# Attention with probabilities and values as half precision pairs, and the second half's keys copied in two parts in the third turn

## The chip, the cores and the metric

The kernel runs on one core of a Trainium2 chip. The metric is the time of one execution on the device, in microseconds; the times given are medians of several runs. The engines are named as in the profile: PE (TensorE, the matmuls), PEld (its weight loads, which overlap PE), DVE (VectorE), ACT (ScalarE), POOL (GpSimd) and SP (SyncE, whose queue issues most DMAs).

## What is computed

Two layers of an encoder for 256 prompt tokens and 64 sample tokens (T = 320 together). Each layer has a projection, latent attention with 8 heads, an mLSTM branch, a gated MLP branch, their gated sum, and a mixture of 16 experts. The change touches the attention alone:

```python
def _attend_block(qn, qr, qpos, kn, kr, v, kpos):
    s = jnp.einsum('bqhd,bkhd->bhqk', qn, kn) + jnp.einsum('bqhd,bkd->bhqk', qr, kr)
    s = s.astype(jnp.float32) * ATTN_SCALE
    allowed = (kpos // CHUNK)[None, :] <= (qpos // CHUNK)[:, None]
    s = jnp.where(allowed[None, None], s, -jnp.inf)
    p = jax.nn.softmax(s, axis=-1)
    return jnp.einsum('bhqk,bkhd->bqhd', p.astype(v.dtype), v)
...
    for l in range(DEPTH):
        z = x @ w_in[l] + b_in[l]
        cq, ckv, kr, mq, mk, mv, mi, mf, mo, gu, gv, gt = _split(z)
        q = (_rmsnorm(cq, q_norm_g[l]) @ w_uq[l]).reshape(B, T, MLA_HEADS, NOPE_DIM + ROPE_DIM)
...
        kv = (ckv_all @ w_ukv[l]).reshape(B, past + T, MLA_HEADS, NOPE_DIM + V_DIM)
        a_out = _mla_attention(qn, qr, positions, kv[..., :NOPE_DIM], kr_all, kv[..., NOPE_DIM:], kpos)
...
        merged = jax.nn.sigmoid(gt[..., :D_MODEL]) * (a_out @ w_branch[l, 0])
...
        x = _layernorm(DN_ALPHA * x + merged @ w_out[l], ln1_g[l], ln1_b[l])
        moe_out = _moe(x, router_w, router_b, moe_w_gate[l], moe_w_up[l], moe_w_down[l],
                       shared_w_gate[l], shared_w_up[l], shared_w_down[l])
        x = _layernorm(DN_ALPHA * x + moe_out, ln2_g[l], ln2_b[l])
```

The 256 prompt tokens see only prompt tokens up to their own chunk of 64; the 64 sample tokens see 256 cached tokens and themselves.

## The kernel before

The engines have hand-written programs, joined by semaphores (`Signal`: a semaphore and its count per layer). Activations lie transposed, 128 features on the partitions and the 320 tokens in the free dimension.

**Weights** come as blocks of 128 x 1024 f32, 358 in all, over SP's queue into eight buffers `w32`. ACT writes the upper half of a block's bits as f16 into `whi` (`hi_at`, L555), DVE the rest into `wlo` (`lo_at`, L1074); each has four slots. A matmul of full precision is then three f16 matmuls: hi x hi, hi x lo, lo x hi (`group`, L1777). PE starts a block when DVE's count of low halves reaches it (`ready`), ACT may refill a slot when PE's count `blk_done` has passed it, and SP reloads a `w32` buffer when DVE has read it.

**The attention stage** of a layer has 16 such blocks, A0 to A0 + 15. Blocks 0 and 1 hold the query and key/value projections of heads 0 to 3 ("half 0"), 4 and 5 those of heads 4 to 7 ("half 1"), the other twelve are merge gates, independent of the attention: `gate(a)` is 24 matmuls of 320 columns, and serves as work for PE between the steps of attention. Their results take turns in banks 0 to 3 of the PSUM ("items"); `item_freed` says which copy out of a bank must be done before PE may write it again.

**The loop** has 12 turns, u = 0 to 11. u // 6 is the half, and three turns deal with two heads: u % 3 = 0 and 1 are one head's 256 prompt tokens each, u % 3 = 2 is the 64 sample tokens of both heads (the "short" turn). A unit goes through these steps, each on another engine, with units u, u - 1 and u - 2 under way at once:

- `scores(u)` on PE (L2034, L2041), f32, into bank 4 or 5;
- row maxima on DVE (L1465 to L1470) into `sm`, signal `s_max`;
- `exps(u)` on ACT (L796 to L801): exponentials into `prob`, f32, two buffers, and their sums; signal `p_exp`;
- reciprocal and normalisation on DVE (L1473 to L1481), signal `p_norm`;
- `transposes(u)` on PE (L2051): three f32 transposes into bank 6, signal `t_ps`;
- `probs_out(u)` on ACT (L809 to L814): bank 6 into `prob_t` (in `ysq`), f32, signal `t_sb`;
- `values(u)` on PE (L2068 to L2076), f32, weights `v_kv` (64 wide, one head), into bank 7, signal `o_ps`. After three units `out_hi` (ACT) and `out_lo` (DVE) copy bank 7 into the f16 pair `br_hi`, `br_lo`.

In a turn PE runs scores(u), transposes(u - 1), values(u - 2), and then a block of filler work: `queries(1)` in turn 1, `keys(1)` in turn 2, `vals(1)` in turn 3, a gate block in all others. The copies of these results out of PSUM are `q_out`, `k_out` (four parts of two copies) on ACT, `rotate`, `rotated` and `v_out` on DVE. After the loop come gate(14), transposes(11), values(10), gate(15), values(11), and the branches' output projections, which use bank 0 to 3 in the same way.

## Time and profile before

| | us |
|---|---|
| runs | 1021.13, 1021.45, 1022.71 (median 1021.45) |
| the profiled execution | 1021.76 |
| its span, first to last instruction | 1019.9 |
| PE busy | 979.0 (96%) |
| DVE busy | 806.5 (79%) |
| ACT busy | 655.3 (64%) |
| mean granted PE clock | 0.993 of full speed |

A matmul's record is longer than the time it costs: a matmul of 320 columns has a record of 300 ns, and the next one starts 136 ns later. Costs on PE are therefore read from start to start, or from the chain of work that ended last, where a piece lasts until the next begins. The same holds on a small scale on ACT and DVE, where the next instruction begins some 0.1 us before the record of the last one ends.

### The profile page before, as it was taken

The numbers are of one execution on the slowest core, as the hardware profiler recorded it, in microseconds if no ns is written. First come the engines' busy times: TensorE is split into PE (matmuls) and PEld (weight loads), VectorE is DVE, ScalarE is ACT, GpSimd is POOL, SyncE is SP. The second block draws the span as 40 slices with busy tenths as digits, with TensorE's granted clock in tenths as the row PEclk, the third lists the DMA queues.
The fourth block names the chain that finished last, engine by engine and source line by source line (L and its number), as shares of the span: only waits on it lengthen the run. The fifth ranks groups of instructions, "written<-read, shape, count | busy, mean of one in ns | idle before, by whom it ended". The sixth has DMA issues, their size and how long they took to land.

```text
span 1019.9 us, 24037 instructions
## 1 busy us (share of the span) xinstructions
PE 979.0 (96%) x9862; PEld 757.6 (74%) x9862; DVE 806.5 (79%) x1436; ACT 655.3 (64%) x1057; POOL 0.7 (0%) x10
## 2 busy tenths in 40 slices
PE   8999999999999999999999999999999989999995
PEld 6877777777776799976568777777777768998653
DVE  4796767654689899998888876676448899999986
ACT  5675454754355799876776645556543659987864
POOL 0000000000000000000000000000000000000000
PEclk9999999999999999999999999999999999999998
DMA  9845454423465199998836534442334435999961
GB/s 352 301 170 166 148 151 121 131 83 110 145 222 166 54 322 368 360 361 317 288 125 210 181 124 141 151 146 85 104 124 148 144 102 167 359 364 365 375 233 55
DMA packets 59652, 205.02 MB, mean 201 GB/s; under 512 B 7216, under 2 KB 10348, under 8 KB 59020
## 3 DMA queue, kind: packets, MB, share of 16 engines
q1 hardware_dynamic: 55980, 195.95, 55.8%
q10 hardware_dynamic: 3552, 7.42, 2.1%
q8 instruction: 82, 1.34, 0.5%
q14 instruction: 38, 0.31, 0.1%
HBM read 198.76 MB, written 3.40 MB: 198 GB/s over the span
## 4 chain that ended last, share of the span: by engine, by line
PE 64%; DVE 21%; DVEq 5%; ACT 4%; issue 3%; DMA 1%; SPq 1%; ACTq 0%
PE bank L1777 37%; DVE wlo L1074 12%; PE bank L1801 4%; DVEq L1700 4%; PE bank L2313 3%; ACT whi L555 2%; PE bank L2145 2%; PE bank L1806 1%; PE bank L2000 1%; DMA w<-in_w 1%; DVE mo L1702 1%; PE bank L2034 1%; PE bank L2076 1%; DVE xT L1087 1%; PE bank L2329 1%
## 5 line engine op out<-in xcount | busy, mean ns | idle before, releaser
L1074 DVE SCALAR_TENSOR_TENSOR wlo<-w,whi 128x1024 f16<-128x1024 f32 x358 | 428.9, 1220 | 69.4 <-ACT whi L555 67.9
L555 ACT ACTIVATE whi<-w 128x1024 f16<-128x1024 f32 x358 | 368.8, 1048 | 81.6 <-PE bank L1777 48.1
L1777 PE MATMUL bank<-xhi,whi 128*128 128x320 f16 x688 | 206.2, 300 | 0.7 <-DVE wlo L1074 0.6
L1777 PE MATMUL bank<-xhi,wlo 128*128 128x320 f16 x688 | 205.7, 299 | 0.0
L1777 PE MATMUL bank<-xlo,whi 128*128 128x320 f16 x688 | 205.7, 299 | 0.0
L1777 PE MATMUL bank<-arena_b,whi 128*128 128x112 f16 x2048 | 161.7, 213 | 7.7 <-DVE wlo L1074 6.7
L1777 PEld LDWEIGHTS bank<-arena_b,whi 128*128 128x128 f16 x2048 | 149.5, 98 | 12.8 <-issue 8.6
L1777 PE MATMUL bank<-arena_b,wlo 128*128 128x112 f16 x1024 | 157.3, 213 | 0.0
L1777 PEld LDWEIGHTS bank<-arena_b,wlo 128*128 128x128 f16 x1024 | 100.1, 98 | 0.0
L1777 PEld LDWEIGHTS bank<-xhi,whi 128*128 128x128 f16 x688 | 67.2, 98 | 30.8 <-issue 2.8
L1777 PEld LDWEIGHTS bank<-xhi,wlo 128*128 128x128 f16 x688 | 67.3, 98 | 26.1
L1777 PEld LDWEIGHTS bank<-xlo,whi 128*128 128x128 f16 x688 | 67.4, 98 | 25.6 <-issue 1.4
L1777 PE MATMUL bank<-br_hi,whi 128*128 128x320 f16 x192 | 57.4, 299 | 0.0
L1777 PE MATMUL bank<-br_lo,whi 128*128 128x320 f16 x192 | 57.4, 299 | 0.0
L1777 PE MATMUL bank<-br_hi,wlo 128*128 128x320 f16 x192 | 57.4, 299 | 0.0
L2313 PE MATMUL bank<-whi,arena_a 128*112 128x512 f16 x128 | 48.8, 381 | 1.8 <-DVE wlo L1074 1.8
L2313 PE MATMUL bank<-wlo,arena_a 128*112 128x512 f16 x128 | 48.5, 379 | 0.0
L2313 PE MATMUL bank<-whi,arena_b 128*112 128x512 f16 x128 | 48.5, 379 | 0.0
L1801 PE MATMUL bank<-whi,xhi 128*128 128x128 f16 x256 | 44.9, 222 | 2.6 <-ACT x_tail L628 2.6
L703 ACT ACTIVATE arena_a<-bank,par_h 128x320 f32<-128x320 f32 x24 | 12.6, 526 | 53.8 <-PE bank L1777 53.8
L1801 PE MATMUL bank<-whi,xlo 128*128 128x128 f16 x256 | 45.0, 222 | 0.0
L1801 PE MATMUL bank<-wlo,xhi 128*128 128x128 f16 x256 | 44.9, 222 | 0.0
(378 smaller groups left out, 1747.4 us busy)
## 6 DMA issues: line engine op xcount, KB each, us to landing
w<-in_w SPq DMA_DIRECT2D x358, 512.0 KB, 4.9
arena_b<-head_rows ACTq DMA_DIRECT2D x2, 1920.0 KB, 7.3
xT<-in_x SPq DMA_DIRECT2D x2, 640.0 KB, 5.5
out_y<-xT SPq DMA_DIRECT2D x4, 320.0 KB
rows<-in_rows ACTq DMA_DIRECT2D x1, 1024.0 KB, 10.5
rows<-in_rows SPq DMA_DIRECT2D x1, 1024.0 KB, 5.9
out_ckv<-arena_a SPq DMA_DIRECT2D x2, 320.0 KB
acc<-kr SPq DMA_DIRECT2D x2, 288.0 KB
```

The lines of the kernel that those rows point to most:

```text
L555: A(whi[:, n % SLOTS, :], w32[:, n % RAW, :], ACT.Copy, scale=WS).then_inc(hi_done.sem, 1)
L703: A(dst, bank[(M0 + step) % 4][:, 0:T], func, scale=scale, bias=par_t[:, bass.ds(col, 1)]).then_inc(z_ev.sem, 1)
L1074: V.scalar_tensor_tensor(wlo[:, n % SLOTS, :], w32[:, n % RAW, :], WS, whi[:, n % SLOTS, :], ALU.mult, ALU.subtract).then_inc(lo_done.sem, 1)
L1087: V.scalar_tensor_tensor(xT[:, c * T:(c + 1) * T], acc[:, c * T:(c + 1) * T], par_g[:, gain + c:gain + c + 1], ln_r[:, :], ALU.mult, ALU.m ...
L1700: dve.drain()
L1702: V.tensor_tensor(two(h2[:, 0:W2]), two(h1[:, 0:W2]), bank[4 + 2 * e2][:, 0:CAP].unsqueeze(1).broadcast_to([P, 2, CAP]), ALU.mult).then_in ...
L1777: ins = M(out, w[:, s, sub * P:(sub + 1) * P], rhs(part, k), start=(n == 0), stop=(n == 3 * len(subs) - 1))
L1801: M(bank[b][0:m, i * P:(i + 1) * P], x[:, k, t0:t0 + m], w[:, s, k * P:(k + 1) * P], start=(j == 0), stop=(j == 3 * KD - 1))
L1806: ins = M(bank[b][:, 2 * P:3 * P], x_tail[:, k, :], w[:, s, k * P:(k + 1) * P], start=(k == 0 and w is whi), stop=(k == KD - 1 and w is wlo))
L2000: a = M(b[0:m, (i % 2) * 2 * P:(i % 2 + 1) * 2 * P], x[:, k, i * P:i * P + m], w[:, s1, (4 + 2 * k) * P:(6 + 2 * k) * P], start=(j == 0), ...
L2145: a = M(out_bank(c)[:, 0:T], w[:, slot(l, O0 + c), k * P:(k + 1) * P], m[:, k, :], start=(k == 0 and w is whi and m is mhi), stop=(k == KD ...
L2313: a = M(b[0:CAP, :], h_[:, bass.ds(g * (8 * CAP) + ((2 * q + kt) * CAP + H0), CAP)], w[:, slot(l, n), kt * 512:(kt + 1) * 512], start=(q = ...
```

## The change

Probabilities and values become pairs of f16 numbers, as the weights and activations already are.

- `v_kv` becomes `v_hl`: `v_out` is parted into `v_out_hi` on ACT and `v_out_lo` on DVE. `prob` has one buffer; the normalised probabilities are written as `prob_h` (hi by `probs_hi` on ACT, lo by `probs_lo` on DVE, scaled by 4096), `prob_t` as hi by `columns_hi` on ACT and lo by `columns_lo` on DVE. The normalising passes on DVE go; one on the two reciprocals comes.
- `exps(u)` now also waits for `probs_lo(u - 1)`, which frees `prob`; `transposes(u)` waits for `probs_lo(u)`, `values(u)` for `columns_lo(u)`.
- A transpose is two f16 matmuls against the identity that add up in PSUM, values three f16 matmuls where one f32 was (`weigh`).
- On PE the filler block stands ahead of values(u - 2), and these ahead of transposes(u - 1). On ACT and DVE the copy of a transposed unit moves from the next turn to the start of the one after.
- The copies of half 1 move: `q_out(1)` from turn 2 to the end of turn 1, `k_out(1)` from turn 3 to turn 2 in two parts around exps(2), `rotate(1)` from turn 2 to turn 1, `rotated(1)` ahead of the reciprocal of turn 2. `v_out(1)` stays in turn 4.

```diff
+PS = 4096.0
...
-        v_kv = arena_b[:, 8 * T:16 * T].rearrange("p (h i n) -> p h i n", h=2, i=5)
+        v_hl = arena_b[:, 8 * T:16 * T].bitcast(F16).rearrange("p (h a i n) -> p h a i n", h=2, a=2, i=5)
...
-        prob = mu_var[:, 0:6 * P].rearrange("p (b n) -> p b n", b=2)
...
+        prob = mu_var[:, 0:3 * P]
+        prob_h = mu_var[:, 3 * P:9 * P].bitcast(F16).rearrange("p (b a n) -> p b a n", b=2, a=2)
...
+                def v_out_hi(hf):
+                    if hf:
+
+                        act.wait_ge(stored.sem, stored.value(l, 16 * 4))
+                    for n in range(3):
+                        act.wait_ge(*item_done(l, hf, 8 + n))
+                        b = item_bank(ITEM0[hf] + 8 + n)
+                        if n < 2:
+                            a = A(v_hl[:, hf, 0, 2 * n:2 * n + 2, :], b[:, :].rearrange(
+                                "p (i n) -> p i n", i=2), ACT.Copy, scale=UN * XS)
...
                 def exps(u):
                     act.wait_ge(s_max.sem, s_max.value(l, u + 1))
+                    if u:
+                        act.wait_ge(p_lo.sem, p_lo.value(l, u))
...
+                def probs_hi(u):
+                    act.wait_ge(p_inv.sem, p_inv.value(l, u + 1))
                     if u >= 2:
                         act.wait_ge(t_ps.sem, t_ps.value(l, u - 1))
...
+                        A(prob_h[:, u % 2, 0, 0:P], prob[:, 0:P], ACT.Copy, scale=sm[:, 6:7])
+                        A(prob_h[:, u % 2, 0, P:3 * P], prob[:, P:3 * P], ACT.Copy, scale=sm[:, 7:8]
+                          ).then_inc(p_hi.sem, 1)
...
+                def columns_hi(u):
                     act.wait_ge(t_ps.sem, t_ps.value(l, u + 1))
...
+                        A(prob_t[:, u % 2, 0, :], bank[6][:, 0:3 * P], ACT.Copy).then_inc(t_hi.sem, 1)
...
                 hi_a(1)
+                v_out_hi(0)
                 hi_a(2)
                 for u in range(UNITS):
+                    if u >= 2:
+                        columns_hi(u - 2)
+                    if u == 2:
+                        k_out(1, (0, 1))
                     if u in (5, 8, 11):
                         out_hi(u // 3 - 1)
+                    if u == 4:
+                        v_out_hi(1)
+                    elif u not in (2, 3):
+                        gate_tanh(FILLER[u - 1] if u else 2)
+                    exps(u)
                     if u == 2:
-                        q_out(1)
-                    elif u == 3:
-                        k_out(1)
-                    elif u != 4:
-                        gate_tanh(FILLER[u - 1] if u else 2)
-                    if u:
-                        probs_out(u - 1)
-                    exps(u)
+                        k_out(1, (2, 3))
                     if u != 3:
                         hi_a(FILLER[u])
+                    if u == 1:
+                        q_out(1)
+                    probs_hi(u)
...
+                def probs_lo(u):
+
+                    dve.wait_ge(p_hi.sem, p_hi.value(l, u + 1))
+                    if u % 3 < 2:
+                        V.scalar_tensor_tensor(prob_h[:, u % 2, 1, 0:P], prob[:, 0:P], sm[:, 6:7],
+                                               prob_h[:, u % 2, 0, 0:P], ALU.mult, ALU.subtract)
...
+                def columns_lo(u):
+                    dve.wait_ge(t_hi.sem, t_hi.value(l, u + 1))
+                    if u % 3 < 2:
+                        V.tensor_tensor(prob_t[:, u % 2, 1, :], bank[6][:, 0:3 * P], prob_t[:, u % 2, 0, :],
+                                        ALU.subtract).then_inc(t_lo.sem, 1)
...
                 for u in range(UNITS):
+                    if u >= 2:
+                        columns_lo(u - 2)
                     if u in (5, 8, 11):
                         out_lo(u // 3 - 1)
...
+                    if u == 1:
+                        rotate(1)
+                    if u == 2:
+                        rotated(1)
                     dve.wait_ge(p_exp.sem, p_exp.value(l, u + 1))
                     V.reciprocal(sm[:, 6:6 + w], sm[:, 4:4 + w])
                     dve.drain()
...
+                    V.tensor_scalar(sm[:, 6:6 + w], sm[:, 6:6 + w], PS, None, ALU.mult
+                                    ).then_inc(p_inv.sem, 1)
                     if u != 3:
                         lo_a(FILLER[u])
+                    probs_lo(u)
...
                 def transposes(u):
-                    pe.wait_ge(p_norm.sem, p_norm.value(l, u + 1))
+                    pe.wait_ge(p_lo.sem, p_lo.value(l, u + 1))
                     if u:
-                        pe.wait_ge(t_sb.sem, t_sb.value(l, u))
+                        pe.wait_ge(t_lo.sem, t_lo.value(l, u))
                     for i in range(3):
                         n = P if u % 3 < 2 or i < 2 else TS
-                        a = TR(bank[6][0:n, i * P:(i + 1) * P], prob[:, u % 2, i * P:i * P + n],
-                               ident[:, :])
+                        for y in range(2):
+                            a = M(bank[6][0:n, i * P:(i + 1) * P], prob_h[:, u % 2, y, i * P:i * P + n],
+                                  mats16[:, 0, :], start=(y == 0), stop=(y == 1))
                     a.then_inc(t_ps.sem, 1)
...
+                    def weigh(out, kt, rows_, vc, at, first, last):
+                        for x, y in ((0, 0), (0, 1), (1, 0)):
+                            a = M(out, v_hl[0:rows_, hf, x, kt, vc], prob_t[0:rows_, u % 2, y, at],
+                                  start=(first and x == 0 and y == 0), stop=(last and x == 1))
+                        return a
...
                 for u in range(UNITS):
                     scores(u)
-                    if u:
-                        transposes(u - 1)
-                    if u >= 2:
-                        values(u - 2)
                     if u == 1:
                         queries(1)
...
                     else:
                         gate(FILLER[u])
+                    if u >= 2:
+                        values(u - 2)
+                    if u:
+                        transposes(u - 1)
                 gate(14)
+                values(UNITS - 2)
                 transposes(UNITS - 1)
-                values(UNITS - 2)
                 gate(15)
                 values(UNITS - 1)
```

What stands in a row on three engines follows. The names: `bank` is PSUM, `mu_var` holds prob and prob_h, `ysq` prob_t, `arena_b` the queries and the values, `acc` and `arena_c` the keys of half 0 and half 1, `mats16` the f16 identity.

PE in turn 3 of layer 0, before, from the scores of unit 3 to the first matmul of vals(1):

```order
L2034 MATMUL bank5<-acc,arena_b 128x128 [waits p_exp]
L2034 MATMUL bank5<-acc,arena_b 128x256
L2051 MATMUL bank6<-ident,mu_var 128x128 [waits t_sb,p_norm]
L2051 MATMUL bank6<-ident,mu_var 128x128
L2051 MATMUL bank6<-ident,mu_var 64x128
L2068 MATMUL bank7<-ysq,arena_b 64x128 [waits t_sb]
L2069 MATMUL bank7<-ysq,arena_b 64x128
L2071 MATMUL bank7<-ysq,arena_b 64x128
L2000 MATMUL bank2<-whi,kv_hi 128x256 [waits qk_ev]
```

PE in turn 3 after, from the end of vals(1) to the scores of unit 4:

```order
L2064 MATMUL bank0<-whi,kv_lo 64x256
L2132 MATMUL bank7<-ysq,arena_b 64x128 [waits t_lo]
L2132 MATMUL bank7<-ysq,arena_b 64x128 x8
L2116 MATMUL bank6<-mats16,mu_var 128x128 [waits t_lo,p_lo]
L2116 MATMUL bank6<-mats16,mu_var 128x128 x3
L2116 MATMUL bank6<-mats16,mu_var 64x128 x2
L2098 MATMUL bank4<-acc,arena_b 128x128 [waits p_exp]
L2098 MATMUL bank4<-acc,arena_b 128x256
```

The three transposes and three f32 matmuls of values have moved behind vals(1), values first, as six and nine f16 matmuls; the transposes of unit 2 end with two 64 wide ones, and the scores of unit 4 follow them.

ACT in turns 1 to 3 before, from the query copies (64x320) to the copy of the transposed unit 2:

```order
L770 ACTIVATE arena_b<-bank 64x320 x4
L809 ACTIVATE ysq<-bank 128x384
L801 ACTIVATE mu_var,sm<-bank,sm 128x320
L555 ACTIVATE whi<-w 128x1024
L779 ACTIVATE arena_c<-bank 64x288 x8
L812 ACTIVATE ysq<-bank 128x256
L814 ACTIVATE ysq<-bank 64x128
L796 ACTIVATE mu_var,sm<-bank,sm 128x128
```

ACT after, from the query copies to the copy of the transposed unit 1, which is the last row:

```order
L561 ACTIVATE whi<-w 128x1024
L776 ACTIVATE arena_b<-bank 64x320 x4
L829 ACTIVATE mu_var<-mu_var,sm 128x128
L830 ACTIVATE mu_var<-mu_var,sm 128x256
L841 ACTIVATE ysq<-bank 128x384
L785 ACTIVATE arena_c<-bank 64x288 x4
L821 ACTIVATE mu_var,sm<-bank,sm 128x320
L785 ACTIVATE arena_c<-bank 64x288 x4
L561 ACTIVATE whi<-w 128x1024
L833 ACTIVATE mu_var<-mu_var,sm 128x320
L841 ACTIVATE ysq<-bank 128x384
```

The query copies have moved ahead of the high half of unit 1 (L829, L830), the key copies (64x288) ahead of the weights' high half (L555, now L561), four before and four behind the exponential of unit 2. The copy of the transposed unit 1, second in the rows of before, is last.

DVE in turn 2 before, from the rotation products to the maxima of unit 3:

```order
L1414 SCALAR_TENSOR_TENSOR mq<-bank2,cosT 128x320 [waits qkv_ps]
L1414 SCALAR_TENSOR_TENSOR mk<-bank3,sinT 128x320 [waits qkv_ps]
L1468 TENSOR_REDUCE sm<-bank4 128x1 [waits s_ps]
L1470 TENSOR_SCALAR sm<-sm 128x1
L1473 RECIPROCAL sm<-sm 128x1 [waits p_exp]
L1481 TENSOR_SCALAR mu_var<-mu_var,sm 128x320
L1422 TENSOR_TENSOR arena_b<-mq,mk 32x320 x4
L1074 SCALAR_TENSOR_TENSOR wlo<-w32,whi 128x1024 [waits hi_done]
L1465 TENSOR_REDUCE sm<-bank5 128x1 [waits s_ps]
```

DVE after, from the low half of unit 1's probabilities to the maxima of unit 3:

```order
L1490 SCALAR_TENSOR_TENSOR mu_var<-mu_var,sm 128x128 [waits p_hi]
L1492 SCALAR_TENSOR_TENSOR mu_var<-mu_var,sm 128x256
L1503 TENSOR_TENSOR ysq<-bank6,ysq 128x384 [waits t_hi]
L1533 TENSOR_REDUCE sm<-bank4 128x1 [waits s_ps]
L1535 TENSOR_SCALAR sm<-sm 128x1
L1459 TENSOR_TENSOR arena_b<-mq,mk 32x320 x4
L1542 RECIPROCAL sm<-sm 128x1 [waits p_exp]
L1544 TENSOR_SCALAR sm<-sm 128x1
L1111 SCALAR_TENSOR_TENSOR wlo<-w32,whi 128x1024 [waits hi_done]
L1496 SCALAR_TENSOR_TENSOR mu_var<-mu_var,sm 128x320 [waits p_hi]
L1503 TENSOR_TENSOR ysq<-bank6,ysq 128x384 [waits t_hi]
L1530 TENSOR_REDUCE sm<-bank5 128x1 [waits s_ps]
```

The four additions of the rotation (32x320 x4) have moved ahead of the reciprocal of unit 2, and behind the weights' low half (L1074, now L1111) two new subtractions stand ahead of the maxima of unit 3.

## Rows read from the trace of the kernel before

**Rows 1.** The page: busy time of each engine, share of the span, instructions.

```profile
PE 979.0 (96%) x9862; PEld 757.6 (74%) x9862; DVE 806.5 (79%) x1436; ACT 655.3 (64%) x1057; POOL 0.7 (0%) x10
```

**Rows 2.** Chain of waits, in order of time, layer 0: start, us, what.

```profile
185.71 3.26 PE bank L1777 x24
...
200.03 3.50 PE bank L2000 x30
203.53 0.85 PE bank L2034 x4
...
214.69 0.66 PE bank L2034 x4
215.34 0.33 PE bank L2051 x3
215.68 0.36 PE bank L2068 x2
216.04 0.22 PE bank L2069 x2
216.47 3.37 PE bank L1777 x24
...
220.83 1.26 PE bank L2076 x12
...
225.46 0.70 PE bank L2041 x8
226.16 0.48 PE bank L2051 x3
```

**Rows 3.** Timeline of PE: start, length, line, tiles, rows*weight columns, moving data.

```profile
56.01 0.22 PE L1806 MATMUL bank<-whi,x_tail 128*128 128x128 f16 x1
56.06 0.22 PE L1806 MATMUL bank<-wlo,x_tail 128*128 128x128 f16 x1
...
202.49 0.27 PE L2000 MATMUL bank<-whi,kv_lo 128*128 128x256 f16 x1
202.69 0.30 PE L2000 MATMUL bank<-whi,kv_hi 128*64 128x256 f16 x1
202.82 0.27 PE L2000 MATMUL bank<-wlo,kv_hi 128*64 128x256 f16 x1
...
352.12 0.32 PE L2268 MATMUL bank<-mats,arena_a 128*112 128x128 f16 x3 [1.11 <-ACT arena_b L948]
352.27 0.26 PE L1777 MATMUL bank<-arena_b,whi 128*128 128x112 f16 x2
```

**Rows 4.** Timeline of ACT, turns 1 to 3 of layer 0: same columns.

```profile
189.99 0.49 ACT L809 ACTIVATE ysq<-bank 128x384 f32<-128x384 f32 x1 [0.46 <-PE bank L2051]
190.86 0.37 ACT L796 ACTIVATE mu_var<-bank,sm 128x128 f32<-128x128 f32 x1 [0.37 <-DVE sm L1470]
...
191.66 1.05 ACT L555 ACTIVATE whi<-w 128x1024 f16<-128x1024 f32 x1
192.61 1.76 ACT L770 ACTIVATE arena_b<-bank 64x320 f32<-64x320 f32 x4
...
195.43 0.53 ACT L801 ACTIVATE mu_var<-bank,sm 128x320 f32<-128x320 f32 x1 [0.50 <-DVE sm L1470]
...
196.90 3.35 ACT L779 ACTIVATE arena_c<-bank 64x288 f32<-64x288 f32 x8
```

**Rows 5.** Timeline of DVE, turn 1 into turn 2 of layer 0.

```profile
192.75 1.23 DVE L1074 SCALAR_TENSOR_TENSOR wlo<-w,whi 128x1024 f16<-128x1024 f32 x1 [0.15 <-ACT whi L555]
193.89 0.48 DVE L1414 SCALAR_TENSOR_TENSOR mq<-bank,cosT 128x320 f32<-128x320 f32 x1
```

**Rows 6.** Stretches: length, busy PE, PEld, DVE, ACT, POOL, PE clock, DMA.

```profile
184.00:256.00 72.00, 72.00 (x547) 52.79 (x546) 38.36 (x90) 41.06 (x98) 0.00 (x0) 1.00 0.34 111
327.70:341.00 13.30, 13.29 (x147) 9.61 (x148) 10.66 (x33) 6.74 (x13) 0.00 (x0) 0.87 0.09 34
828.70:840.80 12.10, 11.91 (x147) 9.06 (x148) 10.67 (x33) 6.73 (x13) 0.00 (x0) 1.00 0.09 36
```

More of the change, by code:

```diff
@@ L322, in build_trunk @@
         q_rot = sig("q_rot", 2)
+        v_hi = sig("v_hi", 6)
         v_ev = sig("v_ev", 6)
@@ L772, in q_out, with k_out @@
                         a.then_inc(qk_ev.sem, 1)
-                def k_out(hf):
-                    for n in range(4):
+                def k_out(hf, parts=range(4)):
+                    for n in parts:
                         act.wait_ge(*item_done(l, hf, 4 + n))
@@ L843, in _ @@
                 gate_tanh(14)
[L844 removed]
+                columns_hi(UNITS - 1)
                 hi_a(15)
```

110 lines of the change are left out of this document (59 added, 51 removed).

## The prediction

> **What bounds the kernel now.** I read the page's first part first: TensorE (PE) is busy 979.0 of 1019.9 us, VectorE (DVE) 806.5, ScalarE (ACT) 655.3 [rows 1]. A share of the whole says nothing of one stage, so next comes the chain of work that ended last, taken in order of time over the attention of layer 0 (about 172 to 256 us). It holds nothing but PE: scores, transposes, values, the 24 matmuls of a gate block, and again, each piece ending where the next begins [rows 2]. So here a microsecond off PE is one off the kernel, provided that ACT and DVE still deliver in time. Last come the rows of ACT and DVE in the same stretch [rows 4, 5], since that proviso is what the change puts at risk. Layer 1 repeats the pattern. In what follows u = 0 to 11 is the turn of the loop; turn 2 is the "third turn". Turns of heads take u % 3 = 0 or 1; the turn of the short sequence ("short turn") has u % 3 = 2.
>
> **PE: values.** In f32 one head's values are three matmuls in two passes each: 0.36 (L2068) + 0.22 (L2069) + 0.22 (L2071, like it) = 0.80 us [rows 2]. They become nine f16 matmuls of 128 columns with 64 wide weights. f16 matmuls of 128 columns start 0.056 apart (L1806) [rows 3], so nine are 0.50. A change of weight width costs extra on PE: from 128 to 64 wide the start moves 0.20 on where 0.11 is usual, and the next one stands 0.13 on, in all 0.12 (L2000) [rows 3]. Values are then 0.62 for a head. The short turn has 12 passes in 1.26 [rows 2]; it becomes 18 matmuls of 64 columns. Such a one behind 112 wide weights let the next start in about 0.03: the three of L2268 and the start of L1777 span 0.15 [rows 3]. 18 x 0.03 = 0.52, and four changes of tile are 0.48: 1.00.
>
> **PE: transposes.** Three f32 transposes take 0.33 [rows 2]; six f16 matmuls against the identity are 6 x 0.056 = 0.34. But they now stand behind the values, not between 128 wide work, so each group pays the change of width on entry: 0.45. Before, only those behind the scores of the short turn paid that (0.48 [rows 2]). The transposes of a short unit end with two 64 wide matmuls. As matmuls of 64 wide f16 weights they are like L2000's tail, which pays on both sides: 0.12 more on entry, and the scores behind them take 0.85 instead of 0.66, as the scores do behind L2000's tail [rows 2]. In exchange the gate block behind the values (3.37) starts behind the scores and is back at 3.26 [rows 2], except in short turns.
>
> **PE: the sum.** Three turns before: (0.66 + 0.33 + 0.80 + 3.37) + (0.66 + 0.33 + 1.26 + 3.37) + (0.70 + 0.48 + 0.80 + 3.37) = 16.13. After: (0.85 + 3.26 + 0.62 + 0.57) + (0.66 + 3.26 + 1.00 + 0.45) + (0.70 + 3.37 + 0.62 + 0.45) = 15.81. Saved 0.32 for three turns, about 0.95 for turns 3 to 11. Turn 2 saves 0.18 + 0.03 = 0.2, and the tail (gate 14, values 10, transposes 11, gate 15, values 11) 9.13 - 8.82 = 0.3. Together 1.4 us of PE a layer.
>
> **ACT and DVE: what is added.** Per unit: ACT gets the high half of the probabilities (128 and 256 columns); DVE gets their low half and the low half of the transposed block, and loses the two normalising passes. No row has these. The copy lies between one copy of 384 columns (0.49) and the two exponentials with their reads (0.80) [rows 4]; without reads it is nearer the former: 0.55, and 0.61 until DVE sees it. The DVE pair lies between 0.48 (one pass of 320 columns [rows 5]) and twice that; I take 0.61. The low half of the transposed block has 384 columns where that row has 320: 0.55. Halving v moves 1.4 us a half to ACT; DVE keeps its 1.6. The stage gives ACT and DVE 41.1 and 38.4 busy us in 72 [rows 6], and with some 9 and 8 us more they still fit. What doesn't fit is local. The gate copies of turns 4 and later wait for PE, and there is slack of 0.5 us or more before each set of values. The first half of the loop is where queries and keys of half 1 are copied.
>
> **Where PE will wait.** The low half of unit 0 now stands ahead of DVE's maximum of unit 1, so ACT's exponentials of turn 1 start at 190.86 + 0.53 = 191.4. From there ACT is never idle: exponentials 0.80, weights 0.95, q copies 1.76 (to 194.9) (L796, L555, L770) [rows 4], probabilities of unit 1 0.55 (195.45), block of unit 0 0.39 (195.85), keys part 0 and 1 1.69 (197.5), exponential of unit 2 0.53 (198.05; L801) [rows 4], keys part 2 and 3 1.69 (199.7), weights 1.05 (200.8). DVE: the weights' low half 1.14 [rows 5], low half of unit 2 0.45, of block 1 0.5: 202.9. PE wants exactly that block (values of unit 1) when vals(1) ends. Before, turn 4's scores began at 203.5 [rows 2]; less 0.33 and 0.80 that no longer stand in front, less 0.2 of turn 2 and 0.11 of width in vals(1), and some 0.1 because a piece of the chain begins with the end of the one before, a little behind the first start, it is 202.0. So PE waits about 0.9 in turn 3. The delay goes on: unit 3's exponentials start near 203.7, the v halves follow, unit 4's start near 209.2, and block 3 with out_lo(0), for which values of unit 3 wait, is done at about 213.7, within 0.1 of PE. From turn 6 on the slack is back. Net per layer 1.4 - 0.9 = 0.5 saved; both layers 1.0. The rest of the program moves with PE, since weight loads wait for DVE's count of finished blocks. The profiled execution took 1021.76 for a span of 1019.9, and stands 0.3 over the median; from the median the forecast is 1021.45 - 1.0 = **1020.4**. About 0.2% (2.0 us) is what a measurement of this kernel can tell from no change, so this is "no change".
>
> **Rival 1, clearly faster.** The two 64 wide transposes pay nothing, as the f32 ones do now (their 0.33 is the same for short units [rows 2]), or the copies are at the low end. The first gives 4 x 0.12 + 3 x 0.19 = 1.05 us a layer, of which the waits take back some 0.35; the second shortens the wait by 0.3. Together a layer saves 0.5 + 0.7 + 0.3 = 1.5: 1018.4. Against it stands L2000's row, which has just this form.
>
> **Rival 2, slower.** The hand-overs between ACT and DVE are what ends last, in more than one turn. Values of unit 0 have only 0.2 of slack. If the copy costs what the exponentials do and DVE's pair 0.8, units 0, 1 and 3 wait 0.5 + 1.1 + 0.9, net -1.1 a layer; with a further 0.1 for each hand-over -1.4, giving 1024.2. It outweighs the PE saving once the waits of a layer exceed 1.4. For it: ACT's row of work in turns 1 and 2 has no gap left. Against it: most of its links are measured here.
>
> **Rival 3, 64 wide f16 weights don't hide behind their matmul.** A matmul of 64 columns then takes what an f32 pass of 64 takes now: (1.26 less four changes of about 0.14) / 12 = 0.06 [rows 2]. The short turns' values are 0.56 dearer, 2.2 a layer, 0.4 of it taken out of the wait: net -1.3 a layer, 1024.0. If those of 128 columns too take as long as an f32 pass, 0.11 [rows 2], 8 x 0.49 = 3.9 a layer come on top: 1031.9. L2268's 112 wide weights speak against both, with three starts in 0.15 [rows 3].
> The Trainium skill, TensorE: Matmul & The Clock Gate, section "Weight-path perf modes — Fast Weight Load (FWL) and DoubleRow", says that the fast load works only for a full 128 columns of a type that isn't f32. Its section "LDWEIGHTS (loading the stationary operand)" gives columns / 1.2 ns, so 53 ns for 64: by the page these loads just hide behind 128 columns and not behind 64, which would make 18 x 0.053 = 0.95 instead of 0.52 and, an estimate, 1023 for the whole. The trace has no f16 matmul with 64 wide weights and fewer than 256 columns, so no run here shows it yet.
>
> **Clock.** The same router stretch took 13.30 us at a granted clock of 0.87 in layer 0 and 12.10 at 1.00 in layer 1 [rows 6], behind the same layer norm. A shift of the work may add or drop such a stretch of 1.2 GHz: 1.2 us either way.
>
> **How the numbers follow.** Forecast 0.57, rival 1 0.22, rival 2 0.10, rival 3 0.07 (0.05 of it the cheaper form), a clock stretch more or less as the deciding thing 0.04. Faster by over 0.2% (under 1019.4): rival 1 and half of the clock, and a little of the forecast's own edge, 0.25. Slower (over 1023.5): rivals 2 and 3, 0.17. Within: 0.58. The range takes in rival 1 at 1018.4 and the cheaper form of rival 3 at 1024.0, with most of rival 2: 1018.2 to 1024.0; what is outside is the dear form of rival 3 and the tails of rivals 1 and 2, less than 0.2.
>
> **What would show it.** Transposes and values in f16 with starts 0.056 apart, 0.62 for a head's values, 1.00 for the short turn's; 0.57 and 0.85 around the 64 wide transposes; one PE wait of about 0.9 before the values of unit 1 with DVE's subtraction as its releaser, and none over 0.3 elsewhere; ACT without a gap from 191.4 to 200.8. Starts 0.1 apart in the values, or waits in turns 2 and 5 as well, would make it wrong on the slow side; no wait in turn 3 on the fast side.

## The result: 0.44% slower, and outside the range

The changed kernel takes 1025.28 us (median of six runs, 1022.35 to 1027.63) where the kernel before takes 1020.98 in the runs beside it: a ratio of 1.0044, 95% interval 1.0033 to 1.0056. The forecast was 1020.4, "no change", with a range up to 1024.0. So the sign was wrong, and the time was out of the range by 1.3.

First the page of the changed kernel, the rows that answer to [rows 1] and the row of the queue that brings PE's instructions (packets, MB, share):

```profile
PE 975.3 (96%) x10030; PEld 754.4 (74%) x10030; DVE 823.2 (81%) x1492; ACT 672.5 (66%) x1109; POOL 0.7 (0%) x10
...
q8 instruction: 84, 1.38, 0.5%
```

PE is 3.7 us less busy, and the kernel is longer. So the loss must be sought in idle time and in the granted clock, over the whole span.

**The attention of layer 0** comes first. The chain of waits in order of time, as in [rows 2]:

```profile
183.18 0.66 PE bank L2098 x4
...
195.95 0.03 ACT mu_var L821
...
198.13 0.96 ACT whi L561
...
199.11 1.23 DVE wlo L1111
200.33 0.46 DVEq L1534
200.79 0.48 DVE ysq L1503
...
201.31 0.69 PE bank L2132 x9
202.00 0.56 PE bank L2116 x6
202.56 0.85 PE bank L2098 x4
203.41 3.26 PE bank L1841 x24
206.68 1.02 PE bank L2132 x18
...
209.79 1.22 DVE wlo L1111
...
212.15 0.41 DVE br_lo L1482
...
212.69 0.66 PE bank L2132 x9
...
254.34 5.67 PE bank L1841 x41
```

[Rows 2] held nothing but PE. Now ACT and DVE are in the chain twice, and both times the piece ahead of PE's is a low half on DVE that stood behind the weights' low half (`wlo`, 1.2 us). PE's own timeline around the values of units 0, 1 and 3 (start, length, line, tiles):

```profile
194.81 0.29 PE L1841 MATMUL bank<-kv_hi,wlo 128*128 128x288 f16 x1
195.16 0.69 PE L2132 MATMUL bank<-ysq,arena_b 128*64 128x128 f16 x9
...
200.12 0.27 PE L2064 MATMUL bank<-whi,kv_lo 128*64 128x256 f16 x1
201.31 0.69 PE L2132 MATMUL bank<-ysq,arena_b 128*64 128x128 f16 x9 [0.92 <-DVE ysq L1503]
...
211.91 0.30 PE L1841 MATMUL bank<-xhi,wlo 128*128 128x320 f16 x1
212.69 0.66 PE L2132 MATMUL bank<-ysq,arena_b 128*64 128x128 f16 x9 [0.48 <-DVE br_lo L1482]
```

The usual distance over such a change of width is 0.23. What is over it is wait: 0.12, 0.96 and 0.55, together 1.63 us. From the first scores to the first matmul of the output projections the stage takes 71.26 us, where the kernel before took 70.97; layer 1 gives 71.27 and 70.96. So the attention costs 0.30 a layer, 0.6 in all, and PE's own saving in it is 1.63 - 0.30 = 1.33. (This counts the values as starting 0.23 behind the work ahead of them. after_early_shift48, below, shows that in turn 3 they can start sooner, so the wait there costs more than 0.96.)

**The other place** lies outside the stage. PE at the start of layer 1, in the first block after the layer norm:

```profile
509.30 0.30 PE L1902 MATMUL bank<-xhi,whi 128*128 128x320 f16 x1 [1.68 <-ACT xhi L581]
...
510.11 0.30 PE L1902 MATMUL bank<-xhi,whi 128*128 128x320 f16 x1
512.94 0.30 PE L1902 MATMUL bank<-xhi,wlo 128*128 128x320 f16 x1 [2.53 <-issue]
```

Seven matmuls after it has restarted, PE stands for 2.53 us with nothing to wait for: "issue". The kernel before runs through here. The same 71 matmuls in both kernels, before and then after (stretch, length, busy PE, PEld, DVE, ACT, POOL, granted clock, DMA), and the part of it behind the gap:

```profile
512.10:522.90 10.80, 10.40 (x71) 6.50 (x72) 9.57 (x20) 6.85 (x14) 0.00 (x0) 1.00 0.15 49
```

```profile
509.30:523.30 14.00, 11.47 (x71) 7.52 (x72) 10.15 (x21) 7.72 (x16) 0.00 (x0) 0.88 0.22 75
...
513.70:517.20 3.50, 3.50 (x16) 1.93 (x15) 3.50 (x8) 1.11 (x4) 0.00 (x0) 0.51 0.04 9
```

The stretch is 3.3 us longer (14.01 for 10.76 by the starts). After standing for 2.5 us PE was granted 1.2 GHz for 3.4 us. With the attention that is 3.3 + 0.6 = 3.9 of the 4.5 that the ratio gives.

The profiled execution itself was the shortest of six (1022.35). The kernel before had two stretches at half clock that it lacks:

```profile
28.70:32.20 3.50, 3.50 (x37) 3.50 (x35) 3.20 (x6) 3.15 (x6) 0.00 (x0) 0.51 1.03 411
329.10:332.60 3.50, 3.50 (x27) 2.11 (x25) 3.42 (x9) 2.44 (x6) 0.00 (x0) 0.51 0.00 1
```

```profile
28.70:32.20 3.50, 3.50 (x45) 3.10 (x43) 3.09 (x8) 3.47 (x6) 0.00 (x0) 1.00 1.02 407
329.10:332.60 3.50, 3.50 (x44) 2.62 (x42) 3.42 (x8) 3.02 (x5) 0.00 (x0) 1.00 0.00 0
```

The second one can be priced: from the end of layer 0's attention stage to the start of layer 1 PE takes 256.31 us in the kernel before, 255.03 in the changed one and 255.12 in before_shift168, which has no such stretch. The changed kernel's execution is also 1.88 us ahead when the first scores start. The first stretch doesn't explain that, since shift224 has none there either and is no earlier than the kernel before (184.90 and 184.89). Together these two favour the changed kernel's profiled execution by some 3 us. Of the twelve profiled executions in this document seven have the first stretch, two the second, and three one near 830 us in layer 1; each comes in some executions and not in others of nearly the same program, so none of it is put down to the change.

ACT's rows in turn 1, needed below: the high halves of a head's probabilities (128 and 256 columns) and the block behind them.

```profile
193.07 0.39 ACT L829 ACTIVATE mu_var<-mu_var,sm 128x128 f16<-128x128 f32 x1
193.36 0.50 ACT L830 ACTIVATE mu_var<-mu_var,sm 128x256 f16<-128x256 f32 x1
193.88 0.49 ACT L841 ACTIVATE ysq<-bank 128x384 f16<-128x384 f32 x1
```

### The profile page after: what moved, and what is told of

Read it like the earlier page. It is cut to its first block, busy times and chain, and to the rows that moved or that the text cites. A ratio compares the mean times of both kernels' runs of the same rounds, so it can differ in the third digit from the quotient of the medians.

```text
span 1020.6 us, 24505 instructions
## 1 busy us (share of the span) xinstructions
PE 975.3 (96%) x10030; PEld 754.4 (74%) x10030; DVE 823.2 (81%) x1492; ACT 672.5 (66%) x1109; POOL 0.7 (0%) x10
## 3 DMA queue, kind: packets, MB, share of 16 engines
q8 instruction: 84, 1.38, 0.5%
## 4 chain that ended last, share of the span: by engine, by line
PE 62%; DVE 21%; DVEq 6%; ACT 5%; issue 3%; DMA 1%; SPq 1%; ACTq 0%
PE bank L1841 36%; DVE wlo L1111 12%; PE bank L1865 4%; DVEq L1764 4%; PE bank L2382 3%; ACT whi L561 3%; PE bank L2132 2%; PE bank L2214 2%; PE bank L1870 1%; DVE mo L1766 1%; DMA w<-in_w 1%; PE bank L2098 1%; PE bank L2116 1%; DVE xT L1124 1%; PE bank L1910 1%
## 5 line engine op out<-in xcount | busy, mean ns | idle before, releaser
L1111 DVE SCALAR_TENSOR_TENSOR wlo<-w,whi 128x1024 f16<-128x1024 f32 x358 | 429.2, 1220 | 77.0 <-ACT whi L561 75.7
L561 ACT ACTIVATE whi<-w 128x1024 f16<-128x1024 f32 x358 | 368.8, 1048 | 82.5 <-PE bank L1841 48.1
## 6 DMA issues: line engine op xcount, KB each, us to landing
rows<-in_rows ACTq DMA_DIRECT2D x1, 1024.0 KB, 10.2
rows<-in_rows SPq DMA_DIRECT2D x1, 1024.0 KB, 7.4
```

The costliest lines, as they stand in the source:

```text
L561: A(whi[:, n % SLOTS, :], w32[:, n % RAW, :], ACT.Copy, scale=WS).then_inc(hi_done.sem, 1)
L1111: V.scalar_tensor_tensor(wlo[:, n % SLOTS, :], w32[:, n % RAW, :], WS, whi[:, n % SLOTS, :], ALU.mult, ALU.subtract).then_inc(lo_done.sem, 1)
```

## The experiments

**The theories.** F: PE's instructions come in pieces of 16 KB (the 84 packets of 1.38 MB above). One matmul with its weight load is two instructions. Between the layers PE jumps over the code for the case that the tokens of an expert don't fit. An instruction of the compiled program has 64 bytes, so a piece holds 256. The places that follow are counted in that program, and stand in no trace. The jump lands on instruction 11,053 before and 11,221 after (168 more: 84 more matmuls a layer), and the next multiple of 256 is 11,264: 211 instructions ahead before, 43 after. The changed kernel would run out of the piece that it jumped into before the next one is there. The Trainium skill, Runtime: NRT & Kernel Launch, section "Instruction fetch mechanics", says that instructions are refilled in blocks of 16 KiB, 256 of them, and that a taken branch breaks the sequential prefetch when its target isn't in the pages at hand. The trace agrees with a stall at the jump: its record on PE's sequencer lasts 3.50 us (504.77 to 508.27), with a packet of instructions 0.9 us into it. It is hidden behind 16 unread matmuls and the wait for the layer norm: PE restarts 4.53 or 4.54 us after the jump in all the kernels below, though this record lasts from 3.26 to 3.92. The gap is a second stall, 7 matmuls behind the restart. A: the attention costs it all, more in most executions than in the profiled one. R: the gap was a chance of one execution.

Each ratio is to the runs of the kernel before on the same chip in the same set of runs, so the medians of different rows don't compare. There is one profiled execution of each kernel. In all that follows "the stage" is the time from the first scores to the first matmul of the output projections, the same within 0.02 in both layers, and "the restart" the time from the first matmul of layer 1 to the 24th of the low passes behind it. "shift48" means 24 matmuls in the branch that isn't taken. They are never executed.

| kernel | median us | ratio to before, 95% | stage | restart |
|---|---|---|---|---|
| before | 1020.98 | 1 | 70.97 | 10.76 |
| changed | 1025.28 | 1.0044 (1.0033 to 1.0056) | 71.26 | 14.01 |
| after_shift48 | 1021.82 | 1.0018 (1.0008 to 1.0029) | 71.27 | 10.76 |
| before_shift168 | 1024.85 | 1.0056 (1.0042 to 1.0070) | 70.96 | 14.29 |
| shift224 | 1022.33 | 1.0018 (1.0007 to 1.0030) | 71.25 | 10.76 |
| before_ksplit | 1022.30 | 1.0019 (1.0008 to 1.0029) | 71.93 | 10.76 |
| kwhole_shift48 | 1026.95 | 1.0052 (1.0035 to 1.0069) | 73.63 | 10.75 |
| after_early | 1024.10 | 1.0046 (1.0033 to 1.0059) | 70.45 | 14.66 |
| after_early_shift48 | 1020.12 | 1.0005 (0.9995 to 1.0016) | 70.48 | 10.76 |
| early2_shift48 | 1019.78 | 0.9996 (0.9985 to 1.0006) | 70.47 | 10.75 |
| wide_shift48 | 1019.81 | 0.9998 (0.9989 to 1.0007) | 70.51 | 10.75 |
| early3_wide_shift48 | 1018.98 | 0.9978 (0.9968 to 0.9989) | 69.82 | 10.76 |

### after_shift48: the same work, the code moved

```diff
                 with pe.Else():
+                    if l == 0:
+                        unread(6, 24)
                     pe.sem_inc(xg_ps.sem, 4 * GROUPS)
```

(`unread(b, n)` is n matmuls into bank b that nothing reads.)

> The changed kernel with 24 matmuls (48 instructions: each has a weight load) put into the branch of layer 0 that is not taken (more tokens for an expert than fit). They are never executed; they only move everything behind that branch by 48 instructions in the compiled program. Theory F (instruction fetch): the 2.8 us for which PE stands at 510 us, between two matmuls of the first block of layer 1 with nothing to wait for, come from the 16 KB piece in which PE's instructions are fetched: the jump over the untaken branch now lands some 20 instructions ahead of the end of a piece, and the next piece comes too late. Moved by 48 instructions the jump lands at the start of a piece: the gap is gone, the stretch at half clock that follows it as well, and the time falls by 2.7 to 4.3, from 1025.3 to 1021.0 to 1022.6. Theory A (the attention stage costs it all: waits that the profiled execution happened to miss): the time stays at 1025.3 within 0.5. Theory R (a stray stall of one execution): the gap is gone or not as it happens, and the time stays at 1025.3.

Measured: ratio 1.0018, no gap, restart 10.76. As F has it: moving code that nobody executes took off 2.6 thousandths, 2.7 us, the low end of what was expected; A falls as the whole cost, and R falls. The stage is unchanged.

### before_shift168: the gap made in the kernel before

The same edit in the kernel before, with `unread(6, 84)`.

> The kernel before, with 84 matmuls (168 instructions) in the branch of layer 0 that is not taken, so that the code behind it stands where it stands in the changed kernel (the change added 84 matmuls with their loads ahead of it). Nothing of it is executed. Theory F: the gap of some 2.7 us appears behind the jump, in the seventh or eighth matmul of layer 1's first block, mostly with half clock behind it: 1021.0 + 2.7 to 4.3 = 1023.7 to 1025.3, though nothing of the attention is changed. Theories A and R: 1021.0 within 0.5, no gap.

Measured: ratio 1.0056, with the gap at the same seventh matmul and half clock behind it. PE's timeline, and the stretch behind the gap:

```profile
512.23 0.30 PE L1838 MATMUL bank<-xhi,whi 128*128 128x320 f16 x1
514.12 0.42 PE L1838 MATMUL bank<-xhi,wlo 128*128 128x320 f16 x1 [1.60 <-issue]
```

```profile
513.20:520.10 6.90, 5.98 (x23) 3.34 (x23) 6.83 (x16) 3.51 (x6) 0.00 (x0) 0.51 0.03 11
```

The restart takes 14.29, 3.5 more. The gap is shorter here (1.60) and the time at 1.2 GHz longer (6.8 us), so the price is about the same. after_early, below, has the jump in the same place too: the gap is 2.45, the time at 1.2 GHz 6.8, the restart 14.66, 3.9 more. The ratio (5.7 us, with 4.3 as its lower end) is 2.2 us more than the trace shows. That stays open.

### shift224: how far the jump must be from the boundary

As after_shift48, with `unread(6, 112)`: the jump lands on 11,445, 75 instructions ahead of a multiple of 256 instead of 43.

> As after_shift48, but with 112 matmuls (224 instructions) in the untaken branch. The jump then lands 32 instructions further from the next 16 KB boundary of PE's program than in the changed kernel: 16 matmuls more (2.2 us) are in the piece that is there. In the two executions with the gap PE stood still 7 matmuls after it had restarted, and went on 3.6 (changed kernel) and 2.7 us (before_shift168) after the restart. Theory F with a fixed delay (the next piece is asked for only after the restart, and takes 2.7 to 3.6 us until its first matmul): 23 matmuls last 3.1 us, so 0 to 0.5 of the gap is left: ratio 1.0018 to 1.0025. Rival (the fetch starts only when the piece in hand is nearly used up): the gap has its full 1.6 to 2.5 us, 23 matmuls in, ratio 1.004.

Measured: ratio 1.0018, restart 10.76. PE runs out of instructions 23 matmuls in, as worked out, for a moment only:

```profile
514.37 0.30 PE L1902 MATMUL bank<-xhi,whi 128*128 128x320 f16 x1
514.73 0.30 PE L1902 MATMUL bank<-xhi,wlo 128*128 128x320 f16 x1
```

0.36 from start to start, 0.23 over the usual, and a wait for the next activations takes even this back. The following piece gives its first matmul 3.6 us (changed kernel, 509.30 to 512.94), 2.7 (before_shift168) and 3.6 (here, 511.16 to 514.73) after the restart, so it doesn't wait for the instructions in hand to run out. Why 3.6 and 2.7 is seen in the instruction queue. These are its rows in the changed kernel for 505.6 to 510.4, where the piece that the jump lands in comes, and for 510.6 to 511.6 (packets, MB, share):

```profile
q8 instruction: 1, 0.02, 1.5%
q8 instruction: 1, 0.02, 5.6%
```

The second packet starts 1.33 us after the restart in the changed kernel, 0.28 in before_shift168, 1.07 in after_early and 1.27 here, takes 0.9 to 1.0, and the first matmul behind it starts another 1.41, 1.40, 1.60 and 1.41 later. In all twelve kernels of the table, those without a gap too, this packet starts between 0.5 before and 1.4 after the restart, which is 4.0 to 5.9 us after the jump. What sets it off, and why it varies, stays open. 23 matmuls behind the restart cover the delay but for 0.06 us, 7 don't. With their loads these are 47 and 15 instructions, 28 fewer both times than the compiled count says (75 and 43); no run shows why.

### before_ksplit: the second part of the change alone

```diff
                     if u == 2:
-                        q_out(1)
-                    elif u == 3:
-                        k_out(1)
-                    elif u != 4:
+                        k_out(1, (0, 1))
+                    elif u not in (3, 4):
                         gate_tanh(FILLER[u - 1] if u else 2)
                     if u:
                         probs_out(u - 1)
                     exps(u)
+                    if u == 2:
+                        k_out(1, (2, 3))
                     if u != 3:
                         hi_a(FILLER[u])
+                    if u == 1:
+                        q_out(1)
```

and on DVE `rotate(1)` in turn 1, `rotated(1)` ahead of the reciprocal of turn 2.

> The kernel before with the second part of the change alone: the second half's queries are copied and rotated in turn 1 (rotation added up in turn 2), its keys in two parts in turn 2 around the exponentials, in the order that the changed kernel has. Values, probabilities and PE's program are as before. Theory: in the kernel before PE waits nowhere in these turns, so moving ACT's and DVE's work is worth nothing as long as no wait appears: ratio 1.000 within 0.0007. Rival (the new place itself makes PE wait, since ACT's turns 1 and 2 are fuller; then part of the 1.6 us of waits seen in the changed kernel belongs to this part and not to the half precision pairs): a wait of 0.3 to 1.0 a layer, ratio 1.0006 to 1.002.

Measured: ratio 1.0019, stage + 0.96. The rival holds, at its upper end: PE waits before the transposes of unit 2, since two parts of the keys now stand ahead of that unit's exponentials.

```profile
198.55 0.82 PE L2036 MATMUL bank<-acc,arena_b 98*128 98x128 f32 x4
199.96 0.55 PE L2053 MATMUL bank<-ident,mu_var 128*128 128x128 f32 x3 [0.59 <-DVE mu_var L1485]
```

### kwhole_shift48: the first part of the change alone

The changed kernel with `q_out(1)` in turn 2, `k_out(1)` whole in turn 3, `rotate(1)` and `rotated(1)` in turn 2.

> As after_shift48, with the second part of the change undone: queries of half 1 are copied in turn 2 and rotated there, its keys in one piece at the start of turn 3, as in the kernel before; the half precision pairs stay. In before_ksplit the new place alone made PE wait 0.75 us before the transposes of unit 2 and cost 1.0 a layer. Theory K (the new place of the copies is also what makes the changed kernel wait before the values of units 1 and 3): these waits go, 0.5 to 1.5 a layer are saved, ratio 1.0018 becomes 0.999 to 1.0008. Rival (with the pairs, ACT is on the way in each turn, and the keys in one piece, 3.4 us, put unit 3's exponentials late, so the new place is what the pairs need): a wait of 1 us or more appears before the transposes or the values of unit 3 or 4, ratio 1.0018 or above, up to 1.004.

Measured: ratio 1.0052, stage + 2.66. Theory K was right in one point: the waits before the values of units 1 and 3 are gone. The time is still far worse, and not where either theory had looked: PE waits before it can write the keys at all, since the rotation product on DVE (`mq`), which has to read the queries out of the bank first, is late.

```profile
194.25 0.77 PE L2103 MATMUL bank<-acc,arena_b 98*64 98x256 f32 x8
197.40 0.40 PE L1839 MATMUL bank<-kv_hi,whi 128*128 128x288 f16 x1 [2.38 <-DVE mq L1449]
```

From the last 0.6 us of this wait on PE is granted 1.2 GHz, for 3.4 us, and likewise in layer 1:

```profile
196.80:200.20 3.40, 2.80 (x12) 1.75 (x13) 2.46 (x9) 2.28 (x5) 0.00 (x0) 0.50 0.42 145
```

The keys take 4.45 us instead of 3.06, so about half of the 2.66 is the clock. PE also waits 0.58 for a copy of the keys before vals(1).

So each part alone costs 0.96 and 2.66 a layer, and both together 0.30. The split of the copies was bad for the old order and is needed by the new one. A part tried alone says nothing of its worth in the whole.

### after_early and after_early_shift48: the order on ACT and DVE

On ACT, and the same with `_lo` on DVE:

```diff
-                    if u >= 2:
+                    if u >= 2 and u not in (3, 5):
                         columns_hi(u - 2)
...
-                    if u in (5, 8, 11):
+                    if u in (8, 11):
                         out_hi(u // 3 - 1)
...
+                    if u in (2, 4):
+                        columns_hi(u - 1)
+                    if u == 4:
+                        out_hi(0)
                     if u != 3:
                         hi_a(FILLER[u])
```

> The changed kernel; in turn 2 both halves of unit 1's transposed block, and in turn 4 those of unit 3's block and the copies of the first pair's outputs, are taken ahead of that turn's weight copies on ACT and DVE instead of at the start of the next turn. By the trace the waits before the values of units 1 and 3 (0.96 and 0.55 us) end with DVE's low halves, which stand behind the weights' low half (1.2 us). Theory W (these two waits are the attention's loss): both go to 0.1 or less, a layer saves 1.4 to 1.5, both 2.8 to 3.0: 1025.3 becomes 1022.4. Rival (the same work late somewhere else: the weights' halves and the exponentials behind them come 0.8 later, and scores, transposes 4 or a weight block waits instead): under 1.0 saved.

> Both edits together. If F and W hold they add: 1025.3 - 2.9 - (2.7 to 4.3) = 1018.1 to 1019.7, below the kernel before (1021.0) by 1.3 to 2.9. If the fetch gap has no part in it: 1022.4. If neither holds: 1025.3.

Measured: the stage falls by 0.8 in both, not by 1.5. Both waits went, and two new ones came, 0.87 before the transposes of unit 2 and 0.2 before those of unit 4. In after_early_shift48:

```profile
202.75 0.27 PE L2072 MATMUL bank<-whi,kv_lo 128*64 128x256 f16 x1
202.76 0.30 PE L2140 MATMUL bank<-ysq,arena_b 128*64 128x128 f16 x2
...
203.08 0.27 PE L2072 MATMUL bank<-whi,kv_lo 128*64 128x256 f16 x1
203.12 0.33 PE L2140 MATMUL bank<-ysq,arena_b 128*64 128x128 f16 x3
...
204.32 0.63 PE L2124 MATMUL bank<-mats,mu_var 128*128 128x128 f16 x6 [0.87 <-DVE mu_var L1500]
```

That is the rival. The first rows show one thing more. Where PE doesn't wait, the nine matmuls of the values (L2140) run in between the last six of vals(1) (L2072) and not behind them. Both have 64 columns of weights, and by the kernel the one writes partitions 0 to 63 of its bank and the other 64 to 127. From the first of the six to the last of the nine it is 0.72 us here and in the four other kernels without this wait, and 2.23 in the changed kernel, in both layers. So the wait of turn 3 cost 1.51 and not 0.96, and the sum closes: 1.51 and 0.55 went, 0.94 and 0.30 came, which leaves 0.82.

Without the shift the gap stands at 511.5 us as in the changed kernel (2.45 us), and the ratio shows no gain (1.0046 for 1.0044); with it the two edits add in the stage and in the restart. The ratio of 1.0005 is some 1.5 us above what the trace shows (stage 2 x -0.49).

### early2_shift48: one step on

`probs_hi(2)` and `probs_lo(2)` also go ahead of the weights' copies of turn 2.

> As after_early_shift48, and in turn 2 both halves of unit 2's probabilities are also taken ahead of that turn's weight copies. In after_early_shift48 the wait before the values of unit 1 had gone, and one of 0.87 stood in its place two steps on, before the transposes of unit 2, whose low half stood behind the same weights' low half. Theory W (the wait is a matter of order alone: ACT and DVE have room): no PE wait over 0.2 is left in turns 2 to 5, a layer saves 0.8 to 0.9 more, ratio to the kernel before 1.0005 - 0.0017 = 0.999. Rival (ACT and DVE are really full in turns 2 to 4, so that it only moves on again, to the transposes or values of a later unit): the ratio stays at 1.0005.

Measured: stage 70.47, no gain over 70.48, though the ratio is 0.9 thousandths lower. The wait moved again, and split:

```profile
208.00 0.38 PE L2146 MATMUL bank<-ysq,arena_b 128*64 128x64 f16 x6 [0.50 <-DVE ysq L1515]
...
214.82 0.51 PE L2130 MATMUL bank<-mats,mu_var 128*128 128x128 f16 x6 [0.60 <-DVE mu_var L1499]
```

The transposes of unit 2 start 0.94 earlier, the values of unit 2 lose 0.57 of it and the transposes of unit 4 the rest. So in turns 2 to 5 it isn't one step that is late, it is the sequence of hand-overs from maxima to exponentials to the two halves.

### wide_shift48: the price of a narrow transpose

```diff
-                        n = P if u % 3 < 2 or i < 2 else TS
+                        n = P
```

> As after_shift48, and the third transpose of a short unit takes 128 columns of the probabilities instead of 64 (the 64 columns beyond the 320 are left from an earlier unit, and what they give is read by nothing). Nothing else changes. Theory T (a change of the weights' width costs on both of its sides, as the sum of the prediction has it): the transposes of short units fall from 0.56 to 0.44 and the scores behind them from 0.85 to 0.71, 0.26 for each of four units, three of which have scores behind them; turn 3's is hidden in no wait. 0.9 a layer, part of which the wait before the values of unit 3 takes back: 0.4 to 0.9 a layer, 0.8 to 1.8 in all; ratio 1.0018 becomes 1.0001 to 1.0010. Rival (the width costs nothing, what is seen there is the f32 scores' own entry): 0.56 and 0.85 stay, ratio 1.0018.

Measured: ratio 0.9998, stage - 0.76. The chain of waits over the short unit 5:

```profile
220.10 0.62 PE bank L2132 x9
220.72 0.44 PE bank L2116 x6
221.16 0.71 PE bank L2098 x4
```

0.44 and 0.71 stand where the changed kernel has 0.56 and 0.85. More work (128 columns of weights instead of 64) takes 0.26 less for each short unit with scores behind it. Theory T holds: the stage lies in its range, the ratio slightly below it (0.9998 for 1.0001 to 1.0010). The last short unit saves 0.12 on its transposes and 0.1 on the gate block behind them, so a layer could save 0.26 x 3 + 0.22 = 1.0; the wait before the values of unit 3 took 0.26 back (distance 1.04 instead of 0.78).

### early3_wide_shift48: together

`early2`, `n = P`, and in turn 4 too the probabilities ahead of the weights.

> The edits together: jump moved by 48 instructions, third transposes 128 wide, and in turns 2 and 4 the transposed block of the unit before, in turn 4 the first pair's outputs, and in both turns the unit's own probabilities are taken ahead of the weight copies. early2_shift48 had left waits of 0.57 before the values of unit 2 and 0.60 before the transposes of unit 4; the latter's low half now stands ahead of the weights. Theory (order alone): a layer stands at early2_shift48's -0.5 against the kernel before, -0.8 for the width, -0.5 for the wait in turn 5, that is -1.8, less what the waits take back; both layers -2.4 to -3.6: ratio 0.9965 to 0.9977. Rival (the chain of maxima, exponentials and the pair's two halves is itself as long as PE's turn, so what PE saves comes back as waits): ratio 0.998 to 0.9996.

Measured: ratio 0.9978, 95% 0.9968 to 0.9989: 2.2 us faster than the kernel before, 6.7 than the changed one. The stage is 69.82, 1.15 below before, at the border between the two expectations; two waits are left:

```profile
208.27 0.22 PE L2146 MATMUL bank<-ysq,arena_b 128*64 128x64 f16 x1 [0.75 <-DVE ysq L1515]
...
219.53 0.47 PE L2146 MATMUL bank<-ysq,arena_b 128*64 128x128 f16 x5 [0.63 <-DVE ysq L1510]
```

## Why the prediction was wrong, step by step

- **PE: values and transposes.** Right. Forecast 0.62, 1.00, 0.45 and 0.57, 0.85, 3.26; measured 0.62, 1.02, 0.44 and 0.56, 0.85, 3.26. Only the scores behind 64 wide values are 0.71, not 0.66. Three turns are 15.86 (224.08 to 239.94 in the chain) for 15.81. The sum of a layer is 1.33 for 1.4. What it lacked is that the values of unit 1 can run in between the last of vals(1), worth another 0.55 that the wait of turn 3 hid. (18 x 0.03 is 0.54, not 0.52; that changes nothing.)
- **The width of the transposes**, taken from L2000's tail against the flat 0.33 of the f32 ones, was right, and wide_shift48 shows it.
- **Rival 3** (64 wide weights don't hide) fell: nine matmuls of 128 columns start 0.056 apart, those of 64 columns 0.031, and 18 of these with four changes take 1.02. By the columns / 1.2 ns that the Trainium skill, TensorE: Matmul & The Clock Gate, section "LDWEIGHTS (loading the stationary operand)", gives for a load, 53 ns for 64 columns, the 18 alone would have been 0.95, and 1.43 with the changes, an estimate; the trace disagrees with its 1.02.
- **The wait in turn 3.** Right in its own terms: 0.96 for 0.9, DVE's subtraction as releaser. (Against values that run in between the last of vals(1) it is 1.51.) With the front 1.88 us earlier (185.05 against 183.18), ACT's row of work was to run from 189.5 to 198.9 and ran from 189.6 to 199.0. Within it the high halves of a head's probabilities cost 0.81 (193.07 to 193.88), as the exponentials do, not 0.55; shorter copies of queries and keys made up for it.
- **The wait in turn 5.** Wrong. "Done at about 213.7, within 0.1 of PE" was DVE's out_lo(0) against the values of unit 3. Shifted by 1.88, DVE was to be ready at 211.8 and PE at about 211.7; DVE was done at 212.6 and PE would have started at 212.14. Here the same 0.26 of the halved probabilities had no cover, and the hand-overs added up: unit 3's exponentials came 0.25 late, unit 4's (207.90) 0.6, out_lo(0) 0.8. The term was 0.1 and measured 0.55. With 0.12 before unit 0 the waits were 1.63 for 0.9, which turned the layer from -0.5 to + 0.30.
- **Rival 2** named this: it outweighs the saving "once the waits of a layer exceed 1.4". They were 1.63. It had 0.10, and it should have had more: it was priced as three copies all at their upper ends, when the upper end of one, carried over three hand-overs, was enough.
- **"The rest of the program moves with PE".** This step failed, and it cost most: 3.3 of 3.9. The sum treated all code outside the attention as unchanged work. It is, but 168 more instructions ahead of it move it against the 16 KB pieces. after_shift48 and before_shift168 show it from both sides. The 84 added matmuls stood in the sum by their time alone. With both errors undone the sum gives 1021.45 - 1.0 + 1.6 + 3.3 = 1025.3. That this is the measured median is partly luck: from the 1020.98 of the runs beside it, it is 1020.98 + 0.6 + 3.3 = 1024.9.
- **What would show it** was too narrow: it named only places in the stage. A gap marked "issue" anywhere in a chain that was pure PE should have been on the list.

What stays open: after_shift48, before_shift168, after_early, after_early_shift48 and shift224 lie 1.2 to 2.2 us above what their stages and restarts give, the changed kernel and the other five within 0.7. The first four share one set of runs of the kernel before, the fastest of all (median 1019.86, where the other sets have 1020.98, 1020.32 and 1020.48), so part of their excess may lie in what they are divided by. Another part may be a wait of PE before its matmuls on `arena_c`, 50 us into layer 1, which took 1.29 us in after_early's execution and 0.2 in shift224's and is absent in the others. One profiled execution of each can't settle it.

## What to carry to other kernels

A change that adds or takes away instructions moves all code behind it. Where a program jumps, look at how many instructions lie between the landing and the end of a 16 KB piece, and read the trace behind each jump for an "issue" gap, before a difference of a few microseconds is put down to the edit; dead code in a branch that isn't taken tests it at no cost. Where two engines hand small pieces to and fro, add up the whole sequence with the upper price of each link, since the last link has no slack of its own; pieces that PE waits for go ahead of bulk work like the weights' copies, but here the waits behind them took back more than half of the gain (1.24 of 2.06). And a matmul with narrower weights can cost more than the full one.

## What the runs showed of the hardware

- Of the instruction fetch: the piece behind the one that a jump lands in came 4.0 to 5.9 us after the jump in twelve executions, and in the four where PE ran out was in use 1.4 to 1.6 us after it had arrived, 2.7 to 3.6 after PE's restart, though PE had waited for the layer norm for 1.7 us just before. With 7 matmuls in hand PE stood for 2.53, 2.45 and 1.60 us, with 23 for 0.06.
- The gap cost more than its length: 3.3, 3.9 and 3.5 us, as the granted clock was at 1.2 GHz for 3.4, 6.8 and 6.8 us, from 0.8 us after the gap in the first and from within it in the other two.
- Matmuls with 64 columns of weights that write different halves of the partitions ran in between each other: six of vals(1) and nine of the values in 0.72 us, in both layers of five kernels. The scores of a short unit's two heads, which are of this kind too, start 0.014 apart in pairs.
- At the end of layer 1 there is a jump too, and no gap: PE has no matmul left behind it in any of the traces.
- Halving a head's probabilities (128 and 256 columns, with a scale read from a tile) takes 0.81 us on ACT and 0.66 on DVE; a short unit's (320 columns) 0.57 and 0.46.
